# S5 preparation in another order on all engines, in a hybrid S5 / differential attention trunk on one core

## The reference, cut to what matters

```
mod = silu(c) @ ada_w[0] + ada_b[0]            # 1024 x 6144, of which the S5 mixer needs shift and scale
u = rms_norm(x, norm_g[0, 0]) * (1 + scale) + shift
bu = u @ bb                                    # per group of 16 channels into 64 complex states
h = scan(lambda_bar, bu)                       # diagonal, over 512 steps in chunks
y = Re(h @ c) + d_skip * u
z = gelu(y)
val, gate = split(z @ w_glu); out = val * sigmoid(gate)
```

## Time and profile before

| | us |
|---|---|
| median of 3 runs | 1324.6 |
| lowest and highest | 1319.28 and 1325.88 |
| the profiled execution | 1322.58 |
| its span, first to last instruction | 1320.8 |
| PE busy | 1236.2 (94%) |
| PE weight loads | 993.6 (75%) |
| DVE, ACT, POOL busy | 779.0, 509.4, 386.3 |
| mean granted clock of PE | 0.970 of full speed |

### The profile page before, as it was taken

How to read it: one execution, slowest core, us unless ns; L and a number is a source line. 1 busy time by engine, 2 the same in 40 slices (tenths; PEclk the granted TensorE clock), 3 DMA queues, 4 the chain that set the end, 5 groups by cost and what they waited for, 6 DMA issues and landing times.

```text
span 1320.8 us, 17867 instructions
## 1 busy us (share of the span) xinstructions
PE 1236.2 (94%) x6557; PEld 993.6 (75%) x6557; DVE 779.0 (59%) x1096; ACT 509.4 (39%) x780; POOL 386.3 (29%) x262
## 2 busy tenths in 40 slices
PE   4967999899999999999999989898999999999995
PEld 2726888788888887888788767576788888878883
DVE  7677777868965444242964777866754444442323
ACT  3353453344433343142333455545253343342311
POOL 4950100234644233000204352500234444440001
PEclk9988999889998999999999999989899999999997
DMA  7578544245843223322133222211022222223311
GB/s 296 196 320 196 192 191 191 96 160 188 290 158 117 74 96 107 117 96 96 49 124 96 80 65 79 65 64 64 33 96 95 95 95 95 95 98 125 102 58 64
DMA packets 26697, 162.21 MB, mean 123 GB/s; under 512 B 4496, under 2 KB 4816, under 8 KB 8400
## 3 DMA queue, kind: packets, MB, share of 16 engines
q1 hardware_dynamic: 25632, 161.15, 34.7%
q10 hardware_dynamic: 1008, 0.28, 0.1%
HBM read 152.76 MB, written 2.10 MB: 117 GB/s over the span
## 4 chain that ended last, share of the span: by engine, by line
PE 75%; DVE 9%; issue 3%; ACT 2%; POOL 0%; DVEq 0%; ACTq 0%
PE psum L1743 16%; PE psum L1745 16%; PE psum L1744 16%; PE psum L1866 6%; PE psum L1868 5%; PE psum L1867 5%; PE psum L1946 1%; PE psum L1921 1%; PE psum L1906 1%; PE psum L1907 1%; PE psum L1908 1%; PE psum L1610 1%; DVE stat L1460 1%; DVE wlo L1182 1%; PE psum L1792 1%
## 5 line engine op out<-in xcount | busy, mean ns | idle before, releaser
L1743 PE MATMUL psum<-hhi,whi 128*128 128x512 f32 x960 | 382.4, 398 | 1.9 <-DVE hlo L1323 1.4
L1745 PE MATMUL psum<-hhi,wlo 128*128 128x512 f32 x960 | 376.5, 392 | 0.0
L1744 PE MATMUL psum<-hlo,whi 128*128 128x512 f32 x960 | 376.3, 392 | 0.0
L1182 DVE TENSOR_TENSOR wlo<-raw,whi 128x2048 fp32r<-128x2048 f32 x81 | 194.5, 2402 | 177.4 <-ACT whi L682 177.4
L682 ACT ACTIVATE whi<-raw 128x2048 fp32r<-128x2048 f32 x80 | 153.1, 1914 | 164.4 <-PE psum L1868 146.1
L536 POOL TENSOR_TENSOR ca<-ca,cb 128x512 f32<-128x512 f32 x44 | 141.9, 3226 | 247.9 <-ACT ca L791 247.9
L1743 PEld LDWEIGHTS psum<-hhi,whi 128*128 128x128 f32 x960 | 181.9, 190 | 42.5 <-issue 2.3
L1745 PEld LDWEIGHTS psum<-hhi,wlo 128*128 128x128 f32 x960 | 181.6, 189 | 38.9
L1744 PEld LDWEIGHTS psum<-hlo,whi 128*128 128x128 f32 x960 | 182.0, 190 | 35.9
L1351 DVE SCALAR_TENSOR_TENSOR ca<-psum,convp,ca 128x511 f32<-128x511 f32 x44 | 33.0, 749 | 218.5 <-ACT ca L787 218.5
L1866 PE MATMUL psum<-ghi,whi 128*128 128x512 f32 x352 | 137.2, 390 | 1.5 <-DVE wlo L1182 1.5
(11 more groups left out here) (335 smaller groups left out, 1674.0 us busy)
## 6 DMA issues: line engine op xcount, KB each, us to landing
raw<-in_units SPq DMA_DIRECT2D x92, 1024.0 KB, 4.8
ada_raw<-in_ada_w SPq DMA_DIRECT2D x24, 1024.0 KB, 8.0
ada_ring<-in_ada_w SPq DMA_DIRECT2D x24, 1024.0 KB, 4.7
qk_sw<-ca SPq DMA_DIRECT2D x32, 128.0 KB, 2.3
u<-in_x_blocks SPq DMA_DIRECT2D x1, 2048.0 KB, 7.8
x<-in_x_t SPq DMA_DIRECT2D x1, 2048.0 KB, 8.5
out_t<-x SPq DMA_DIRECT2D x8, 256.0 KB, 2.0
bc_par<-in_s_bc SPq DMA_DIRECT2D x1, 1024.0 KB, 5.4
```

What stands on the lines that cost most here:

```text
L1182: TT(wlo[:, s, :], raw[:, s, :], whi[:, s, :].bitcast(F32), ALU.subtract).then_inc(split_lo, 1)
L1743: M(out, w_hi, hi[:, k, :], start=(k == 0), stop=False)
L1744: M(out, w_hi, lo[:, k, :], start=False, stop=False)
L1745: return M(out, w_lo, hi[:, k, :], start=False, stop=(k == KT - 1))
```

## The change

On SP, units 20 to 23 are loaded behind Toeplitz pieces 0 and 1. On DVE, groups 2 and 3 of `lb` come behind the root and the four products of u. On ACT, row 0 is copied ahead of group 1, the factors of u are made ahead of group 3, the first 16 scalings are placed four by four between the copies of group 3, the scalings of pieces 2 and 3 come behind the copies of the kernel, row 1 is copied ahead of them, and row 2 behind the Gelu step of piece 0. On PE, the modulation units are dealt out otherwise: three ahead of group 0, two in its middle, three ahead of group 1, then the turn of row 0, three ahead of group 2, two in its middle, the small product, two ahead of group 3 and one behind it; units 16 to 19 come behind `inputs(1)`, `inputs(2)` comes ahead of `local(0)`, units 20 to 23 come behind `carried(0)`, then `local(1)`, `inputs(3)`, `back(0)` and `carried(1)`.

```diff
     sp.dma_start(u[:], a["x_blocks"].rearrange("p (g b) -> p g b", g=GROUPS)).then_inc(u_in, 16)
-    for n in range(N_ADA_PE):
+    for n in range(20):
         load_ada0(n)
...
         load_toeplitz(piece)
+    for n in range(20, N_ADA_PE):
+        load_ada0(n)
     sp.wait_ge(ada_used, N_ADA_PE)
...
-    def copy_inputs(g):
+    def copy_inputs(g, beside=None):
...
               psum[:, n % 2, :].rearrange("p (g k) -> p g k", g=4), ACT.Copy).then_inc(inb_ready, 1)
+            if beside:
+                beside(n)
+    uab = s5s[:, 22:26, :].rearrange("p a g -> p (a g)")
+    def scaled(piece, quarter):
+        act.wait_ge(u_normed, piece + 1)
+        g0 = 2 * PO * piece + 4 * quarter
+        for g in range(g0, g0 + 4):
+            ins = A(u[:, g, :], u[:, g, :], ACT.Identity, scale=uab[:, g:g + 1],
+                    bias=uab[:, GROUPS + g:GROUPS + g + 1])
+        if quarter == 3:
+            ins.then_inc(u_ready, 1)
...
     lb_first(2)
+    copy_row(0)
     copy_inputs(1)
...
     copy_inputs(2)
-    copy_row(0)
-    copy_inputs(3)
     for i, cl in enumerate((cl_re, cl_im)):
         A(cl[:, :, 0, :], bc_par[:, 2 + i], ACT.Copy).then_inc(cl_row0, 1)
-    copy_row(1)
     act.wait_ge(umod_psum, 1)
-    uab = s5s[:, 22:26, :].rearrange("p a g -> p (a g)")
     A(uab, psum[:, 7, P:P + 2 * GROUPS], ACT.Copy).then_inc(uab_ready, 1)
     act.wait_ge(uab_ready, 1)
-    for piece in range(OCTS):
-        act.wait_ge(u_normed, piece + 1)
-        for g in range(2 * PO * piece, 2 * PO * (piece + 1)):
-            ins = A(u[:, g, :], u[:, g, :], ACT.Identity, scale=uab[:, g:g + 1],
-                    bias=uab[:, GROUPS + g:GROUPS + g + 1])
-        ins.then_inc(u_ready, 1)
-        if piece == 2:
-            act.wait_ge(k_psum, 1)
-            for b in range(4):
-                A(kx[:, :, 4 * b:4 * b + 4, :].rearrange("p k j c -> p j k c"),
-                  psum[:, 3 + b, :].rearrange("p (j k c) -> p j k c", j=4, k=BL),
-                  ACT.Copy).then_inc(k_copied, 1)
-    copy_row(2)
+    copy_inputs(3, partial(scaled, 0))
+    for quarter in range(4):
+        scaled(1, quarter)
+    copy_row(1)
+    act.wait_ge(k_psum, 1)
+    for b in range(4):
+        A(kx[:, :, 4 * b:4 * b + 4, :].rearrange("p k j c -> p j k c"),
+          psum[:, 3 + b, :].rearrange("p (j k c) -> p j k c", j=4, k=BL),
+          ACT.Copy).then_inc(k_copied, 1)
+    for piece in range(2, OCTS):
+        for quarter in range(4):
+            scaled(piece, quarter)
...
         z_steps(piece)
+        if piece == 0:
+            copy_row(2)
         zt_steps(piece)
...
     signal(bb_ready)
-    for g in range(OCTS):
-        lb_group(g)
+    lb_group(0)
+    lb_group(1)
...
            ALU.mult).then_inc(u_normed, 1)
+    lb_group(2)
+    lb_group(3)
...
     pe.wait_ge(row_clear, 1)
-    def turned_inputs(g):
+    def turned_inputs(g, ns=range(4)):
...
         pe.wait_ge(lb_row0, 2 * g + 2)
-        for n in range(4):
+        for n in ns:
             wait(pe, inb_ready, 4 * g + n - 1)
...
+    def ada_units(lo, hi):
+        for n in range(lo, hi):
+            ada_unit(n)
     pe.wait_ge(lb_zero, 4)
-    for g in range(OCTS):
-        ada_unit(2 * g)
-        ada_unit(2 * g + 1)
-        turned_inputs(g)
-    for n in range(KT, 12):
-        ada_unit(n)
+    ada_units(0, 3)
+    turned_inputs(0, (0, 1))
+    ada_units(3, 5)
+    turned_inputs(0, (2, 3))
+    ada_units(5, KT)
+    turned_inputs(1)
     pe.wait_ge(u_normed, OCTS)
     turn_row(0)
-    for n in range(12, 16):
-        ada_unit(n)
+    ada_units(KT, 11)
+    turned_inputs(2, (0, 1))
+    ada_units(11, 13)
+    turned_inputs(2, (2, 3))
     pe.wait_ge(umod_rhs, 2)
...
       ca[:, 0, 0:2 * GROUPS], start=True, stop=True).then_inc(umod_psum, 1)
-    for n in range(16, 18):
-        ada_unit(n)
+    ada_units(13, 15)
+    turned_inputs(3)
+    ada_units(15, 16)
     pe.wait_ge(inb_ready, 16)
...
     ins.then_inc(k_psum, 1)
-    for n in range(18, 21):
-        ada_unit(n)
     inputs(1)
-    for n in range(21, N_ADA_PE):
-        ada_unit(n)
+    ada_units(16, 20)
+    inputs(2)
     local(0)
     carried(0)
-    for piece in range(1, OCTS):
-        if piece + 1 < OCTS:
-            inputs(piece + 1)
+    ada_units(20, N_ADA_PE)
+    local(1)
+    inputs(3)
+    back(0)
+    carried(1)
+    for piece in range(2, OCTS):
         local(piece)
...
```

## The result

The changed kernel takes 1315.3 us where the kernel before takes 1324.4, medians of three and of four executions. The ratio on record is 0.9942, 95% interval 0.9922 to 0.9962; the quotient of the two medians alone would be 0.9931. One execution each of after, `e5` and `e7` took 2059 to 3142 us and counts in no figure here. The forecast was 1315.8, with 1310 to 1323.5 as its range. The profiled execution took 1315.29, its span is 1313.5. The first GLU unit starts at 139.97, 5.4 us ahead of the 145.37 of before, where 8.8 were forecast; the rest of the gain does not lie in the stretch that the change touches. So the number is right and one of its terms isn't: that the time came out within 0.5 us of the forecast is luck, and it is added up further down.

A forecast was written before the change was run, and what follows sets the result against it. A chain over all engines before the first GLU unit was taken as the bound, SP's queue decisive. That unit was to come at 136.6 instead of 145.4, 8.8 us earlier: 1324.6 - 8.8 = 1315.8 us, range 1310 to 1323.5.

The forecast's parts named there:

- The walk on PE: PE's new list summed from 28.49: 29.4 + 12.0 + 1.5 = 42.9 us, so unit 15 ends at about 71.4.
- the third of "what is late next": SP's queue: 16 Toeplitz issues of 11.0 us from 86.0, then units 20 to 23; PE free at 111.1.
- The 5.2: Assumed time from unit 20's issue at 97.0, behind the Toeplitz transfers, to its landing: 5.2 us.
- rival B: SP's queue is quicker: unit 23 used at 108.4, first GLU unit at 133.6, 1312.8 us; chance 0.14.
- 25.5 us: Stretch from unit 23 used, at 111.1, to the first GLU unit, at 136.6.
- The two paths: From unit 23 to the first GLU unit: DVE's path ends at 136.0, PE's own at 136.6; the later counts.
- a rival by itself (E): PE's clock is low in all that follows unit 23: first GLU unit at 139.2, 1318.4 us; chance 0.10.
- shifted rigidly: Everything from the first GLU unit on keeps its length, 1175.4 us, and only starts earlier.
- unit 23 is used after 114: Sign against the forecast: PE uses unit 23 later than 114, where 111.1 was forecast.
- the three signs: Forecast wrong if unit 23 is used after 114, the last piece waits for a Toeplitz transfer, or the tail isn't 1175.4.
- rival C: Gain mostly given back in SP's queue: first GLU unit at 139.5 to 143.5, 1318.7 to 1322.7 us; chance 0.16.
- 8.3 us for the K matrix: PE's K matrix starts at 74.8 and takes 8.3 us, giving the first Toeplitz transfer at 86.0.

The follow-up runs named there:

- e5: Changed kernel with units 16 to 19 used right behind inputs(0), 20 to 23 behind inputs(1), all 24 loads ahead of the Toeplitz transfers, ACT reordered: 1305.52 us.
- e7: Changed kernel with the first 16 scalings of u behind all ACT copies of group 3, not between them: 1318.96 us, ratio 0.9984 to the kernel before.
- e8: Changed kernel with DVE's part undone, all four groups of lb ahead of the root: 1333.22 us, ratio 1.0089 to the kernel before.
- e4: Changed kernel with one row of cl moved from POOL to DVE, for an earlier rotation table: 1316.92 us, ratio 0.9961 to the kernel before.
- e2: Kernel before with only SP's part of the change, units 20 to 23 loaded behind the first 16 Toeplitz transfers: 1333.81 us, ratio 1.0100.
- e1: Changed kernel with SP's part undone, all 24 unit loads issued ahead of the Toeplitz transfers: 1316.55 us, ratio 0.9969 to the kernel before.
- e3: Changed kernel with 27 unread filler products on PE ahead of units 20 to 23: 1315.59 us, ratio 0.9950 to the kernel before.
- e10: The changed kernel measured and profiled once more, unchanged, with more rounds: 1315.96 us, ratio 0.9943 to the kernel before.
- e12: Changed kernel with 18 unread filler products on PE ahead of units 20 to 23: 1312.54 us, ratio 0.9919 to the kernel before.
- e9_before_again: The kernel before profiled once more, unchanged: 1319.8 us, one time only.
- e11: The same kernel as e5, run and traced once more: 1306.32 us, ratio 0.9867 to the kernel before.
- e6: Changed kernel with units 16 and 17 early, 20 and 21 in the idle stretch, 22 and 23 between Toeplitz pieces, a cl row on DVE, e5's ACT list: 1306.66 us.

## Why the prediction was right, step by step

**What held.** The walk on PE gave 71.4 for the end of unit 15, it was 71.4. The rescaling was to start at 65 and starts at 65.6; the inputs of piece 0 at 73, they start at 72.6; DVE's first piece at 78.7 by POOL's hand, it is 78.86; the first Toeplitz issue at 86.0, it is 86.52. DVE has no idle time ahead of pieces 1 and 2. `e7` and `e8` show that the ACT and DVE orders carry this, 3.0 and 17.4 us of head, and `e4` that the first piece can't start earlier by a table alone. That SP's queue is decisive also held: `e2`'s head came within 0.6 us of a sum made by the same steps (made after the first result was known), and `e1` moves the head by 3.6 us with this list alone.

**What was mis-sized.** The step that failed is the third of "what is late next", the stretch from the first Toeplitz issue to unit 23's end: forecast 111.1, measured 114.5. Its terms: the issue 0.5 later than forecast and the 16 issues 11.4 instead of 11.0, together 0.9; the first load lands 6.4 after its issue instead of 5.2; the second lands 3.3 behind it, the next two the 2.5 that was taken; unit 23 takes 1.88, the upper of the two bounds, and not 1.4. That is 0.9 + 1.2 + 0.8 + 0.5 = 3.4, the whole difference. The 5.2 was read off loads that were issued ahead of the Toeplitz transfers. Here 16 of them were issued ahead of the loads, the last one landing at 101.4, 3.5 us after the first load's issue; behind them a first load landed 6.4 to 7.3 us after its issue in after, `e3`, `e7`, `e10` and `e12`, while four loads with none ahead start with 4.7 in `e1`. A load's delay is to be read from a row with the same work ahead of it.

Three smaller things were missed beside it and cost nothing here. The list said nothing of the 4.11 us for which `inputs(2)` waits for DVE; PE's idle time for the four units was 5.9 us and not 9. DVE's idle time ahead of its subtraction was 11.62 and not some 9. And rival B's sum is 0.3 us short: 108.4 and 25.5 make 133.9.

**From unit 23 on** the forecast had 25.5 us, and 25.5 it is, by compensation. `local(1)` took 3.68 instead of 2.4, the rest made it up. The two paths were put 0.6 us apart, with PE's the later. In the first trace of after DVE's is the later, by 0.76; in `e10_after_again` it is PE's, where `local(2)` waits 2.21 for the Toeplitz piece and nothing waits for DVE:

```profile
125.73 3.48 PE L1700 MATMUL psum<-toep,u 128*64 128x128 f32 x32 [2.21 <-DMA toep<-kx]
```

So the two are level, and this is why `e12` could not turn a full clock into an earlier head.

**The clock** was a rival by itself (E) and came partly true: 0.77 over 100 to 116, units 22 and 23 at 1.9, `local(1)` 1.7 us above its 1.97, while the inputs behind it were nearly at full level again. The Trainium skill, TensorE: Matmul & The Clock Gate, section on HAM oscillation, describes a kernel with longer waits than these, in which each burst behind a wait for a load starts cold. Here units 22 and 23, behind waits of 1.35 and 0.58 us, are as it says, and units 20 and 21, at 1.04 and 1.15 behind waits of 1.67 and 2.28 us, are not. Nor does the trace of before agree with it as plainly as the prediction says: the wait ahead of 84.6 was for ACT, and two units there took 1.04 behind waits for loads of 1.28 and 1.45 us. No rule on the clock alone gives the time here, since `e12` shows that the loss was hidden.

**The rest of the gain.** The head gives 4.2 to 5.4 us, the medians 7.6 to 9.1. The forecast took the tail as shifted rigidly, and said that a tail unlike 1175.4 would make it wrong. The tail was 1173.5, 1.9 less; `e9_before_again` shows that the kernel before does the same at times. So the traced execution was to take 1313.8 and took 1315.3, 3.4 more by the head and 1.9 less by the tail. The forecast of the median then added 2.0 us, the distance of the traced execution of before from its median; the traced execution of after stands on its median. 3.4 less 1.9 less 2.0 is the 0.5 us by which the forecast was off. The last two are jitter and no merit of the sum, and the small error is luck. Of the medians' gain, 1.8 us in the first pair of traces and 3.6 in the second lie neither in the heads nor in the tails: both traced executions of before were faster than its median. Where these are is left open. The forecast had also named "unit 23 is used after 114" as a sign against it, and it is used at 114.5. So by two of the three signs that it had named the forecast was wrong, though the time fits: for the head it was rival C's lower edge (139.5 to 143.5) that came true, for the time the forecast.

**Where the expected gain went.** 12 us at `inputs(0)` become 8.8 in the forecast and 4.2 to 5.4 in the traces. What is lost is lost in the transfers, which stand idle for 8.9 us and are then wanted by both kinds at once. `e11` takes away the last of these and has 12.2 to 12.8 us of head.

## What to carry to other kernels

Before moving a transfer behind another, list all that want the queue in that stretch: if both orders share it, the gain lies in an idle stretch elsewhere, and what opens it is the consumer that frees the slot, not the queue's order. Time a merge of paths by the later of them, and if they are level, expect an edit to one to give nothing. Where the part behind the edit varies by 2 us and more from run to run, compare traces up to a fixed milestone, and let several rounds of times decide the rest.

## What the runs showed of the hardware

**Small transfers behind large ones.** Toeplitz transfers with no load ahead of them landed in 1.8 to 4.1 us, and the first twelve behind four loads of 1 MB in 5.7 to 9.8. The large ones suffered the other way: 6.4 instead of 4.7 for the first.

**Pauses in the kernel's products.** In the stream of 64 by 16 products PE stopped with nothing to wait for, 2.62 us and 1.47 in the trace of after, 3.70 in `e11`, 3.12 in `e6`; the profile calls it "issue". The kernel before has them too, 2.04 and 2.02 us, so they are inside the forecast's 8.3 us for the K matrix. In both traces the two stand 128 products apart. They lie on the chain to the Toeplitz transfers, and no forecast here had them as a term of their own. Their cause wasn't looked for.

**DVE beside POOL.** The first piece took 11.2 us, from 78.86 to 90.02, the third 10.2 (100.76 to 110.94). Rows of DVE's and POOL's timelines in the kernel after, and last POOL's addition in the kernel before:

```profile
81.38 0.69 DVE L1229 TENSOR_TENSOR v_re<-v_re,ca 128x512 f32<-128x512 f32 x1
...
85.75 1.22 DVE L1245 TENSOR_TENSOR ca<-v_ni,rot_s 128x504 f32<-128x504 f32 x1
...
80.93 3.55 POOL L521 MEMSET toep<- 128x2048 f32 x2
85.16 1.27 POOL L523 TENSOR_TENSOR kx<-kx,cb 128x256 f32<-128x256 f32 x1 [0.68 <-ACT kx L681]
...
98.64 0.73 POOL L521 TENSOR_TENSOR kx<-kx,cb 128x256 f32<-128x256 f32 x1 [14.36 <-ACT kx L672]
```

Beside the clears, which read nothing, an operation of DVE keeps its 0.69; beside POOL's addition it takes 1.22, and the addition takes 1.27 instead of 0.73. An operation of DVE that began 0.01 us ahead of the addition, at 85.15, kept its 0.68. In `e11`, where the addition comes behind the first piece, that piece takes 10.2 us with the clears beside it. The Trainium skill, SBUF — State Buffer, section "Who interferes with whom", says just this: a DVE instruction with two SBUF inputs contends with a GpSimd instruction that reads SBUF, not with one that only writes it. The forecast had put the delay of the first piece at up to the clears' 3.55 us and taken nothing; it was 1 us by another instruction, and hidden as foreseen.
